# Second layer's mixing norm: the context tokens behind the first two evictions and the second pair's weight splits

## The reference

```python
y, yc = token_mix(modulate(rms_norm(h, norm_w[layer, 1]), lm[3], lm[4]),
                  modulate(rms_norm(hc, norm_w[layer, 1]), cm[3], cm[4]), w_in[layer], ...)
# in token_mix: both are multiplied by w_in (1024 x 2048) and cut into
# Fourier, retention q, k, v, gate, attention q, k, v
```

## Time and profile before

| | us |
|---|---|
| median of 3 runs | 2784.41 |
| lowest, highest | 2782.95, 2785.24 |
| the profiled execution's own time | 2781.14 |
| its span | 2779.0 |
| PE busy in it | 2692.2 (97%) |
| DVE busy | 1540.4 (55%) |
| ACT busy | 697.0 (25%) |

### The profile page before, as it was taken

One profiled execution on the slowest core, in us unless ns is written; L12 is line 12 of the kernel. 1 busy time (PEld: TensorE's weight loads), 2 busy tenths in 40 slices (PEclk: granted clock), 3 DMA queues, 4 the chain that ended last, 5 costly groups with the idle time before them and its releaser, 6 DMA issues.

```text
span 2779.0 us, 42188 instructions
## 1 busy us (share of the span) xinstructions
PE 2692.2 (97%) x15515; PEld 2331.0 (84%) x15515; DVE 1540.4 (55%) x2701; ACT 697.0 (25%) x1075; POOL 49.1 (2%) x51
## 2 busy tenths in 40 slices
PE   6999999999989999999999999999999989999998
PEld 4888888888879888888888888888887869888886
DVE  5776477543368377626773677257535466533332
ACT  4111111132247231111111311111113245422222
POOL 0000000000021000000000000000000020000000
PEclk9999999999989999999999999999999999999999
DMA  7877477413200167626762577257422300233332
GB/s 223 194 184 182 112 182 186 118 51 83 61 1 2 46 144 186 164 63 163 185 162 60 125 183 172 70 144 185 121 67 72 83 16 7 80 96 106 91 103 86
DMA packets 485789, 316.89 MB, mean 114 GB/s; under 512 B 30588, under 2 KB 483664, under 8 KB 485712
## 3 DMA queue, kind: packets, MB, share of 16 engines
q1 hardware_dynamic: 485712, 315.88, 44.5%
HBM read 313.73 MB, written 2.10 MB: 114 GB/s over the span
## 4 chain that ended last, share of the span: by engine, by line
PE 91%; DVE 4%; ACT 2%; issue 1%; DMA 1%; SPq 1%; DVEq 0%; ACTq 0%
PE pg L647 79%; PE pg L714 4%; PE p L951 2%; PE pn L935 1%; PE p L662 1%; DVE xlo L1480 1%; PE pg L894 1%; DVE tnorm L1472 1%; ACT whi L1043 0%; PE pg L899 0%; DMA ada_first<-in_w_ada 0%; DVE wlo L1332 0%; ACT qd L1148 0%; PE pg L900 0%; ACT xhi L1115 0%
## 5 line engine op out<-in xcount | busy, mean ns | idle before, releaser
L647 PE MATMUL pg<-xhi,whi 128*128 128x512 f32 x2880 | 801.9, 347 | 8.2 <-DVE wlo L1332 6.2
L647 PE MATMUL pg<-xlo,whi 128*128 128x512 f32 x2880 | 797.7, 345 | 0.0
L647 PE MATMUL pg<-xhi,wlo 128*128 128x512 f32 x2880 | 797.0, 345 | 0.0
L1043 ACT CAST whi<-raw 128x1024 fp32r<-128x1024 f32 (+1 forms) x288 | 321.7, 1118 | 1072.6 <-PE pg L647 1065.2
L1332 DVE TENSOR_TENSOR wlo<-raw,whi 128x1024 fp32r<-128x1024 f32 (+1 forms) x288 | 377.6, 1311 | 349.2 <-ACT whi L1043 346.3
L647 PEld LDWEIGHTS pg<-xhi,whi 128*128 128x128 f32 x2880 | 455.5, 188 | 77.8 <-DVE wlo L1332 7.7
L647 PEld LDWEIGHTS pg<-xhi,wlo 128*128 128x128 f32 x2880 | 456.1, 188 | 70.5
L647 PEld LDWEIGHTS pg<-xlo,whi 128*128 128x128 f32 x2880 | 455.6, 188 | 69.5
L1413 DVE SCALAR_TENSOR_TENSOR part<-ada,cond,part 128x256 f32<-128x256 f32 x960 | 465.3, 485 | 32.7
L1521 DVE SCALAR_TENSOR_TENSOR h<-pg,gcol,h 128x512 f32 (+1 forms) x118 | 71.4, 639 | 452.9 <-PE pg L647 452.9
L647 PE MATMUL pg<-ahi,whi 128*128 128x512 f32 x1100 | 305.9, 346 | 0.0
(11 more groups left out here) (202 smaller groups left out, 2017.3 us busy)
## 6 DMA issues: line engine op xcount, KB each, us to landing
ada<-in_w_ada SPq DMA_DIRECT2D x512, 256.0 KB, 4.1
raw<-in_ffn_w_in SPq DMA_DIRECT2D x176, 512.0 KB, 3.9
raw<-in_ffn_w_out SPq DMA_DIRECT2D x64, 704.0 KB, 4.5
raw<-in_w_in SPq DMA_DIRECT2D x24, 512.0 KB, 4.0
ada_first<-in_w_ada SPq DMA_DIRECT2D x8, 1024.0 KB, 12.0
raw<-in_w_in SPq DMA_DIRECT2D x16, 256.0 KB, 3.6
raw<-in_w_o SPq DMA_DIRECT2D x16, 256.0 KB, 2.7
raw<-in_w_o SPq DMA_DIRECT2D x32, 128.0 KB, 2.9
```

Source lines behind the costliest of these rows:

```text
L647: last = nc.tensor.matmul(pg[s][:, p0:p1], w[:, s, k], v[:, k, p0:p1], start=(k == 0 and n == 0), stop=(k == kt - 1 and n == 2))
L1043: nc.scalar.copy(whi[:, s, 0:nk], raw[:, s, 0:nk]).then_inc(s_whi[s], 1)
```

## The change

In the norm of the second layer's mix, ACT and DVE leave out the context part where it stood. They do it in the loop over the tiles of `win`, behind the eviction of tile 1 and the split for tile 3 (n == 1), ahead of the eviction of tile 2. `norm_scaled` and `norm_low` are the former inner functions `scaled` and `low`. SP's and PE's programs are not touched, and the first layer is as it was.

```diff
+        def late_context(i):
+            kind, l = phases[i][:2]
+            return kind == "win" and win_tokens(l, 0) < TOK
 # ACT, norm
-                for k in range(KD):
-                    shift_hi(1, k)
+                if not late_context(i + 1):
+                    for k in range(KD):
+                        shift_hi(1, k)
+            def norm_context(m):
+                shift = m // 3 * MT + m % 3 * 3 * KD
+                p0, p1 = norm_parts(m)[1]
+                for k in range(KD):
+                    act.wait_ge(s_t, xn_count(m, 1, k))
+                    nc.scalar.activation(xhi[:, k, p0:p1], tnorm[:, k % 4, p0:p1], ACT.Identity,
+                                         bias=mod[:, shift + k, 1:2]).then_inc(s_xh, 1)
 # ACT, loop over the tiles of win
                         split_hi(nxt, s, jn)
+                        if n == 1 and late_context(i):
+                            norm_context(m)
 # DVE
+            def norm_context(m):
+                norm_scaled(m, 1, 0)
+                for k in range(KD):
+                    if k + 1 < KD:
+                        norm_scaled(m, 1, k + 1)
+                    norm_low(m, 1, k)
 # DVE, norm
-                scaled(1, 0)
-                for k in range(KD):
-                    if k + 1 < KD:
-                        scaled(1, k + 1)
-                    low(1, k)
+                if not late_context(i + 1):
+                    norm_context(m)
 # DVE, loop over the tiles of win
                         split_lo(nxt, s, jn)
+                        if n == 1 and late_context(i):
+                            norm_context(m)
```

## The result

The changed kernel takes 2791.16 us (median of 20 runs), the kernel before in the same series 2784.5 us (20 runs): a ratio of 1.0025, with a 95% interval of 1.0019 to 1.0031. It is 6.7 us slower. The forecast was +5.7 us (2790.1 us), slower by 0.20%. The prediction took 0.2% for about the least that a measurement of this kernel can tell from no change; with 20 runs a side the interval is 0.12% wide and lies above 1.

What follows compares the result with a forecast made beforehand. PE, busy for 97% of the span, was taken to bound the kernel. Tile 4's later start (+3.3 us) and low clock (+2.4) sum to +5.7 us on the 2784.41 us median: 2790.1 us, range 2785.0 to 2793.3.

Steps and rivals of the forecast that it cites:

- Part 1: Before tile 2 of the second layer's projection: earlier split shrinks PE's 3.93 us stall to about 0.15; alone gains 6.2 us.
- Part 2: Context part ends 8.0 us later, delaying SP's tables and the weights behind them; tile 4 starts 3.3 us later.
- The rule on ring order: Each DMA engine takes descriptors in ring order, so tile 4's weights wait for the 1.5 MB of tables ahead.
- Part 3: PE resumes at low clock after a 9.4 us stall before tile 4; costs 2.4 us, with 1.6 as lower bound.
- Covered at nothing: Tile 2's eviction, the weights of tiles 5 and 6 and the transform table come in time; no cost.
- the sum: Whole kernel: +3.3 us for tile 4's later start and +2.4 us for low clock make +5.7 us.
- A: Rival: tile 4's weights come in time, PE runs through and the 6.2 us gain stays; 2778.2 us; 5%.
- C: Rival: weight loads of tiles 4 and 5 share the DMA engines, tile 4's landing 1.7 us later; +7.4 us; 10%.
- B: Rival: tile 4's weights overtake the tables in the DMA engines; about +2.2 us, 2786.6 us; 12%.
- D: Rival: the second pair's split isn't early, because another wait holds it; +0 to +1 us; 3%.

Runs made afterwards that it cites:

- e9: e6, with context blocks 0 and 1 left in the norm and 2 to 7 behind the splits for tile 3; ratio 0.9989 to the kernel before.
- e1: The changed kernel, with SP in the second layer issuing tiles 4 and 5's weights ahead of its context wait and both tables; ratio 1.0014 to the kernel before.
- e2: The changed kernel, with the rope table off the norm's buffers and SP waiting only for the last latent block before the tables; ratio 0.9990 to the kernel before.
- e7: The changed kernel, with the transform table (1028 KB) loaded once more behind itself, into a place nobody reads; ratio 1.0035 to the kernel before.
- e8: The kernel before, with the transform table (1028 KB) loaded once more behind itself; ratio 1.0004 to the kernel before.
- e3: The changed kernel, with 40 additional matmuls on TensorE ahead of tile 4 whose result nobody reads; ratio 1.0013 to the kernel before.
- e10: The kernel before, with the rope table in a place of its own and the tables issued at the last latent block; ratio 1.0010 to the kernel before.
- e6: e1, with tile 4's subtraction on DVE put ahead of tile 2's rotation; ratio 0.9986 to the kernel before.

## Why the prediction was right, step by step

**Part 1** (the second pair's split comes first). Forecast: tile 2 starts 0.54 us after tile 1's last matmul (2129.95 less 2129.41), full clock. Measured 0.55, clock 1.00. Its worth was put at 6.2 us. In e9, where nothing takes it back, C is 6.1 us shorter than in the first profile of the kernel before. That profile was a dear one, though (below): over the whole stage e9 is 4.8 to 5.6 us shorter.

**Part 2** (the end of the context part drags SP's queue). Forecast: rope goes out 10.09 us after tile 1's last matmul (2139.50 less 2129.41). Measured 10.13 (2140.73 less 2130.60). Tile 4 was forecast at 20.96 us and came at 21.10. e1 and e2 show that SP's wait and the tables together make the loss, e7 that the bytes ahead count. The rule on ring order that was cited from the Trainium skill (page "DMA: Bandwidth & Descriptors", section "Queues, rings and completion order") agrees with e7 and e8: tile 4's weights land 3.0 us later for 1028 KB more ahead of them.

**Part 3** (low clock). Forecast 2.4 us, with bounds of 1.6 and 2.4. Measured 2.2 in the first profile (tile 4 in 10.66 us against 8.47 at full clock) and 1.6 in the second (10.11). The mechanism held: with PE kept at work (e3) tile 4 ran at clock 1.00. The value taken, the upper bound, was too high in both. It is no true upper bound either: behind e7's stall of 12.4 us tile 4 took 11.33, 2.9 more.

**Covered at nothing.** Held: the changed kernel has no stall behind tile 4's start, and tiles 5 and 6 start right behind.

**How near the sum really was.** Against one profile each, the sum was 5.7 and the part of the stage behind tile 1 gave 5.64. That they agree so well is in part luck: +3.3 came as 3.45 and +2.4 as 2.19, two small misses that cancel. The medians gave 6.7 (5.3 to 8.6 by the interval); 5.7 lies within, so the last microsecond may be scatter. The profiles give a likely reason for it, all the same. Over the whole stage (A + C) the kernel before took 41.86 and 41.13 (e8 and e10, which don't change it there, 41.19 and 41.21), the changed one 47.17 and 48.37. That is a mean of 41.35 against 47.77, +6.4 us. Of these, 4.5 us are up to tile 4's start (mean A + B of 37.4 against 32.9), where the sum had 3.3, and 1.9 are low clock in tile 4, where it had 2.4.

Two things are behind the first. The profiled execution of the kernel before was dear: tile 4 came 0.7 us later in it than in the other three (33.39 against 32.66 to 32.73), by the low clock of tile 2. The prediction named this as a possibility and gave it no place in the likeliest value. And there is a slip that it did not see: tiles 0 and 1 take between 14.9 and 17.2 us over the 14 profiles, mostly by the clock (14.9 in the two profiles at clock 1.00, 17.2 in the two at 0.81, and 15.4 to 16.5 at 0.89 to 0.90). In the kernel before the 3.9 us stall hides that, since tile 2's split hangs on the context part and not on tile 0's end. In the changed kernel eviction, casts, context part, tables and weights all hang on the ends of tiles 0 and 1, so a longer A comes through to tile 4. With the mean A of all 14 profiles (16.0) for the changed kernel's own two, the difference would be about 6.1 us, an estimate. Two profiles of the changed kernel can't prove more.

**Rivals.** A (the gain stays) and C (the two weight loads mix) fell: rope went out after 2140, and the cast started 8.62 us after rope's issue, which leaves no 1.7 us for mixing; tile 5's weights landed 1.7 us behind tile 4's, in order. B would have been 2.2; e1 shows that price, 2.3. D fell with tile 2's start.

## What to carry to other kernels

When work is moved later on one engine, list every queue that waits for its last signal, the DMA queue first: here the loss was not on the engines whose order was changed, but on SyncE, whose wait for the same signal held two tables and the weights behind them. Weights behind a full queue came 3.0 us later for 1028 KB more ahead of them here, and whether that matters is decided by slack: the same megabyte cost tile 4 3 us in one kernel and nothing in the other. The gain of this change was taken by leaving in place as much as the hole holds (two of eight blocks), and by issuing the weights that are needed first ahead of the tables. And where a stall takes up what the code ahead of it varies by, two kernels are compared by lengths counted from ahead of that code (here from tile 0's first matmul), not from its end.

## What the runs showed of the hardware

An idle wait on TensorE can hide a low clock ahead of it: four profiles of that kernel's order (before, before again, e8, e10) differ by up to 2.3 us in tiles 0 and 1 (A, 14.92 to 17.22) and by 0.01 us in the start of tile 2, counted from tile 0's. Taking such a wait away exposes the clock's scatter: in the changed kernel tile 2 started 15.96 us after tile 0 in one profile and 17.73 in the other. The cost of low clock in one profile is one draw: behind the same stall of 9.3 us it was 2.2 us once and 1.6 us once. A transfer of 1028 KB that took 6.1 to 6.4 us in this stage of the other runs took 7.6 to 7.7 in the three profiles (e3, e6, e9) in which TensorE was busy for at least 93% of it at clock 1.00 and weights were issued behind it; the reason is open.
